# Five recurrent turns inside the last tile of the first projection, with the weights and buffers laid out for it

## The reference, cut to what matters

```python
def _layer_a(x, conv_buf, h0, norm_g, w_in, cw, cb, w_gx, b_gx, w_ga, b_ga, lam, w_out):
    u = _rmsnorm(x, norm_g) @ w_in               # first projection
    xb, gate = jnp.split(u, 2, axis=-1)
    xc, new_buf = _causal_conv(xb, conv_buf, cw, cb)
    h, h_last = _rglru(xc, h0, w_gx, b_gx, w_ga, b_ga, lam)      # recurrence
    y = (h * jax.nn.silu(gate.astype(jnp.float32))).astype(x.dtype) @ w_out
    return x + y, ...

def _rglru(u, h0, w_gx, b_gx, w_ga, b_ga, lam):
    uf = u.astype(jnp.float32)
    i_t = jax.nn.sigmoid(_block_diag(u, w_gx, b_gx).astype(jnp.float32))
    r_t = jax.nn.sigmoid(_block_diag(u, w_ga, b_ga).astype(jnp.float32))
    log_a = LRU_C * r_t * jax.nn.log_sigmoid(lam.astype(jnp.float32))
    a = jnp.exp(log_a)
    mult = jnp.sqrt(-jnp.expm1(2.0 * log_a))
    bx = mult * i_t * uf
    ...                                          # scan: h[t] = a[t] * h[t-1] + bx[t]
```

## Time and profile before

| | |
|---|---|
| median of 3 runs | 1619.05 us (1617.78 to 1621.24) |
| the profiled execution's own time | 1617.59 us |
| its span, first to last instruction | 1615.8 us |
| PE busy | 1513.2 us, 94% |
| DVE busy | 1159.9 us, 72% |
| ACT busy | 706.7 us, 44% |
| POOL busy | 336.3 us, 21% |
| mean granted TensorE clock | 0.978 of full speed |

### The profile page before, as it was taken

How to read it: one execution, slowest core, us unless ns; L and a number is a source line. 1 busy time by engine, 2 the same in 40 slices (tenths; PEclk the granted TensorE clock), 3 DMA queues, 4 the chain that set the end, 5 groups by cost and what they waited for, 6 DMA issues and landing times.

```text
span 1615.8 us, 31117 instructions
## 1 busy us (share of the span) xinstructions
PE 1513.2 (94%) x10752; PEld 1439.6 (89%) x10752; DVE 1159.9 (72%) x2212; ACT 706.7 (44%) x1576; POOL 336.3 (21%) x240
## 2 busy tenths in 40 slices
PE   7999999998499999998889999999996899999999
PEld 7999999998489999998879999999994688888888
DVE  7865565677499999998865846648457777777771
ACT  5322132134867667762334424334234444444440
POOL 0000000035565555554321000000122111111110
PEclk9999999999699999999899999999997999999999
DMA  6322122153223333334432212112523343333412
GB/s 239 116 81 68 64 85 67 58 174 112 86 85 106 105 97 103 109 92 158 147 104 72 76 51 81 54 62 76 164 85 104 94 116 92 108 88 102 117 47 79
DMA packets 161967, 158.45 MB, mean 98 GB/s; under 512 B 54832, under 2 KB 154928, under 8 KB 161840
## 3 DMA queue, kind: packets, MB, share of 16 engines
q1 hardware_dynamic: 149712, 147.44, 30.2%
q10 hardware_dynamic: 12128, 9.39, 1.8%
HBM read 102.68 MB, written 54.36 MB: 97 GB/s over the span
## 4 chain that ended last, share of the span: by engine, by line
PE 63%; DVE 18%; issue 7%; ACT 3%; DMA 3%; SPq 1%; POOL 1%; DVEq 0%; ACTq 0%; POOLq 0%
PE bank L651 19%; PE s_banks L651 19%; PE bank L1473 11%; DVE r_th L952 4%; PE s_banks L1410 3%; DVE r_x_hi L976 2%; PE bank L1425 2%; PE bank L1455 2%; PE bank L1213 2%; PE bank L1459 1%; PE bank L635 1%; DVE r_x L972 1%; PE s_banks L1182 1%; ACT m_p L1653 1%; DVE b_qstd L534 1%
## 5 line engine op out<-in xcount | busy, mean ns | idle before, releaser
L705 POOL TENSOR_TENSOR w_lo_a<-w_raw_a,w_hi_a 128x1024 fp32r<-128x1024 f32 x24 | 57.9, 2425 | 706.5 <-ACT w_hi_a L700 706.5
L1653 ACT ACTIVATE m_p<-s_banks,m_nm 128x192 f32<-128x192 f32 (+2 forms) x264 | 106.0, 414 | 182.9 <-DVE m_nm L1524 182.9
L1473 PE MATMUL bank<-m_y_hi,w_hi_a 128*128 128x256 f32 (+1 forms) x512 | 150.2, 293 | 0.6 <-DVE m_out L1584 0.6
L1473 PE MATMUL bank<-m_y_lo,w_hi_a 128*128 128x256 f32 (+1 forms) x512 | 145.5, 284 | 0.0
L1473 PE MATMUL bank<-m_y_hi,w_lo_a 128*128 128x256 f32 (+1 forms) x512 | 145.4, 284 | 0.0
L483 ACT ACTIVATE a_out<-a_out 128x352 f32<-128x352 f32 x48 | 24.0, 500 | 255.5 <-DVE a_out L573 255.5
L651 PE MATMUL bank<-a_hi,w_hi_a 128*128 128x352 f32 x384 | 126.1, 328 | 9.8 <-DVE w_lo_a L705 9.6
L651 PE MATMUL s_banks<-b_hi,w_hi_a 128*128 128x352 f32 x384 | 130.4, 340 | 0.0
L651 PE MATMUL bank<-a_hi,w_lo_a 128*128 128x352 f32 x384 | 124.7, 325 | 0.0
L651 PE MATMUL bank<-a_lo,w_hi_a 128*128 128x352 f32 x384 | 124.6, 324 | 0.0
L651 PE MATMUL s_banks<-b_lo,w_hi_a 128*128 128x352 f32 x384 | 124.1, 323 | 0.0
(11 more groups left out here) (204 smaller groups left out, 4909.5 us busy)
## 6 DMA issues: line engine op xcount, KB each, us to landing
w_raw_a<-weights_dram SPq DMA_DIRECT2D x32, 512.0 KB, 4.6
w_raw_b<-weights_dram SPq DMA_DIRECT2D x18, 512.0 KB, 4.2
sga_dram<-a_out SPq DMA_DIRECT2D x48, 176.0 KB, 1.9
r_xc<-xc_dram SPq DMA_DIRECT2D x32, 264.0 KB, 2.9
r_sg<-sga_dram SPq DMA_DIRECT2D x32, 264.0 KB, 2.8
r_x<-xT_dram SPq DMA_DIRECT2D x64, 132.0 KB, 2.2
x_dram<-r_x SPq DMA_DIRECT2D x64, 132.0 KB, 1.8
b_x<-x_dram SPq DMA_DIRECT2D x48, 176.0 KB, 2.3
```

The lines of the kernel that those rows point to most:

```text
L705: ops.tensor_tensor(low, raw, high.bitcast(F32), ALU.subtract)\
L1473: mm = nc.tensor.matmul(out_bank(ts, blk)[:, 0:width], w[pw][:, kt * P:(kt + 1) * P], (m.y_hi, m.y_lo)[px][tp][:, kt, 0:width], start=(n = ...
L1653: nc.scalar.activation(m.p[:, q, k, v0:192], s_banks[:, 2 * q + e, bp * 192 + v0:(bp + 1) * 192], ACT.Exp, bias=m.nm[:, q, k:k + 1], accum ...
```

## The change

`EARLY` now holds five turns: turn 0 behind step 2 of the last tile, 1 behind 6, 2 behind 8, 3 behind 11, 4 behind 13. DVE does each behind the step before (1, 5, 7, 10, 12), and turn 5 behind step 14. SP's loads for these turns are spread over the last tile (`second`, `third`, `fourth`). The low part of y of turn 5 on POOL waits until the projection's last matmul. There is one more weight place (`SLOTS_B` 7), so that unit `U_GATE` is loaded and split in the first tile; the recurrent buffers are ordered anew, with an 80-column gap. DVE splits 11 further units in the last tile, behind steps 5 to 15, and one more in the first tile; POOL keeps two, behind turns 6 and 7. The decay constants are made behind steps 10 to 15 of the first tile, in six parts. Of the second projection's 16 units, one goes into the new place early, and five instead of four are loaded at the end of the recurrent section.

```diff
-SLOTS_A, SLOTS_B, SLOTS_C = 8, 6, 2
+SLOTS_A, SLOTS_B, SLOTS_C = 8, 7, 2
...
-                if m.first_weights and isinstance(s, int) and s == 1 and j + 6 < VECTOR_UNITS:
+                if m.first_weights and isinstance(s, int) and s == 1 and j + 6 <= 2 * NB:
                     low_part(eng, nc.vector, m.unit + j + 6)
+                if m.first_weights and isinstance(s, int) and s == PN and j >= 5 and U_GATE + j - 4 < VECTOR_UNITS:
+                    low_part(eng, nc.vector, U_GATE + j - 4)
                 after(s, j)
...
-        VECTOR_UNITS = UNITS_IN_A
+        VECTOR_UNITS = U_GATE + 12
...
-        SLOTS_IN_B = (list(range(UNITS_GATE)) + list(range(UNITS_GATE + UNITS_KV, SLOTS_A + SLOTS_B))
-                      + list(range(UNITS_GATE, UNITS_GATE + UNITS_KV)) + [SLOTS_A + SLOTS_B, SLOTS_A + SLOTS_B + 1])
+        SLOTS_IN_A = [15, 16] + list(range(1, 15))
+        SLOTS_IN_B = [14, 0, 1, 2, 3] + list(range(6, 12)) + [4, 5, 12, 13, 15]
...
-        EARLY = {(PN, 9): 0, (PN, 13): 1}
+        EARLY = {(PN, 2): 0, (PN, 6): 1, (PN, 8): 2, (PN, 11): 3, (PN, 13): 4}
...
-            project_sync(eng, a1, {0: start})
-            start_gates()
+            def second():
+                load_branch(1, 0)
+
+            def third():
+                load_branch(1, 1)
+                load_gate(0, 2)
+
+            def fourth():
+                load_branch(1, 2)
+                load_gate(0, 3)
+
+            project_sync(eng, a1, {0: start, 1: start_gates, 7: second, 10: third, 12: fourth})
+            load_gate(1, 0)
             run_steps(eng, 2, RN - 2, RN + 2, body)
-            for u in range(U_B1 + UNITS_GATE + UNITS_OUT_A, U_OUT_B):
+            for u in range(U_B1 + UNITS_GATE + UNITS_OUT_A - 1, U_OUT_B):
                 load_unit(eng, u, r.kv_mm, NB * RN)
...
             def after_project(s, j):
-                if isinstance(s, int) and (s, j) == (PN, NB):
-                    decays(eng)
-                if isinstance(s, int) and (s, j) in ((PN, 7), (PN, 12)):
-                    turn(0, 0, 0 if j == 7 else 1)
+                if isinstance(s, int) and s == 1 and j >= 10:
+                    decays(eng, j - 10)
+                if isinstance(s, int) and (s, j + 1) in EARLY:
+                    early_turn(turn, EARLY[s, j + 1])
+                if isinstance(s, int) and (s, j) == (PN, 14):
+                    early_turn(turn, len(EARLY))
...
+                if isinstance(s, int) and (s, g) == (0, NG - 1):
+                    eng.wait_ge(a1.proj_done, 2 * NB * PN)
...
-            low_units(eng, U_GATE, U_GATE + 7)
-            turn(0, 0, 0)
-            low_units(eng, U_GATE + 7, U_GATE + 11)
-            turn(0, 0, 1)
+            for n in range(len(EARLY)):
+                early_turn(turn, n)
```

More of the change, by code:

```diff
@@ new lines, in decays @@
+            if part == 0:
+                eng.wait_ge(lw_act, 2)
+                step(1, nc.vector.tensor_scalar(tmp, e, 2.0, None, ALU.add))
+                step(2, nc.vector.reciprocal(tmp, tmp))
+                step(3, nc.vector.tensor_tensor(z, e, tmp, ALU.mult))
+                step(4, nc.vector.tensor_tensor(z2, z, z, ALU.mult))
+                step(5, nc.vector.memset(acc, 1.0 / (2 * LW_TERMS + 1)))
+            elif part <= LW_TERMS // 2:
+                for i in range(2):
+                    k = LW_TERMS - 1 - 2 * (part - 1) - i
+                    step(2 * i + 1, nc.vector.tensor_tensor(acc, acc, z2, ALU.mult))
+                    step(2 * i + 2, nc.vector.tensor_scalar(acc, acc, 1.0 / (2 * k + 1), None, ALU.add))
+            else:
+                step(1, nc.vector.tensor_tensor(acc, acc, z, ALU.mult))
+                step(2, nc.vector.tensor_scalar(tmp, vec[:, LAM, :], -1.0, 0.0, ALU.mult, ALU.max))
+                step(3, nc.vector.scalar_tensor_tensor(out=tmp, in0=acc, scalar=2.0, in1=tmp, op0=ALU.mult,
+                                                       op1=ALU.add))
+                nc.vector.tensor_scalar(neg_decay[:, :], tmp, -4.0, None, ALU.mult)
+                nc.vector.tensor_scalar(decay[:, :], tmp, 4.0, None, ALU.mult).then_inc(lw_step, 1)
@@ L782, in back_pair, with early_turn, run_recurrent @@
             return (t, 2 * pair) if known(s, lag, RN - 1 + lag) else None
-        EARLY = {(PN, 9): 0, (PN, 13): 1}
-        def run_recurrent(eng, turn, last, after=None):
+        EARLY = {(PN, 2): 0, (PN, 6): 1, (PN, 8): 2, (PN, 11): 3, (PN, 13): 4}
+        def early_turn(turn, n):
+            s, g = divmod(n, NG)
+            turn(s, s % 2, g)
+        def run_recurrent(eng, turn, done, last, after=None):
             def body(s, par):
                 for g in range(NG):
-                    if not (isinstance(s, int) and s == 0 and g < len(EARLY)):
+                    if not (isinstance(s, int) and NG * s + g < done):
                         turn(s, par, g)
@@ L853, in body @@
                         load_branch(s + 1, g - 2)
+                    if isinstance(s, int) and (s, g) == (RN - 1, 0):
+                        load_unit(eng, U_B1)
                     if isinstance(s, int) and (s, g) == (RN, 0):
-                        for k in range(UNITS_GATE):
+                        for k in range(1, 1 + UNITS_GATE):
                             load_unit(eng, U_B1 + k, r.gates_done, 4 * NG * RN)
@@ L859, in body @@
                         load_next(pair, 0)
-                    if known(s, 0, RN - 1) and not (isinstance(s, int) and s == 0 and g < 2):
+                    if known(s, 0, RN - 1):
                         load_gate(s, g)
@@ L887, in start @@
                 eng.wait_ge(a1.proj_done, 2 * NB * (PN - 1))
[L888 to L889 removed]
+                for j in range(4):
+                    eng.wait_ge(a1.stored[place(a1, j)], stored_before(a1, 2, j))
                 for g in range(NG):
```

70 lines of the change are left out of this document (28 added, 42 removed).

## The result

The changed kernel takes 1597.97 us in the median (1597.15 to 1599.24), against 1618.93 us for the kernel before (1617.78 to 1621.24) in runs on the same chip. The ratio is 0.9869 with a 95% interval of 0.9852 to 0.9887: 21 us faster, where the forecast was 12.

A forecast was written before the change was run, and what follows sets the result against it. The prediction took the stretch from 409 to 433 us as a chain of latencies, the gain being how much earlier DVE reaches turn 7. Terms -11.5 - 2.0 + 1.5 = -12.0 gave 1605.6, median 1607.0 us, range 1599 to 1614.

The forecast's parts named there:

- A: The forecast itself: DVE gets to turn 7 earlier, median 1607.0 us, 1603 to 1611 by its bounds; chance 0.62.
- the ring: Last tile, from turn 3 on: DVE and ACT each wait for the other in turn, 14.4 us a turn.
- everything moves as a block: Behind DVE's start of turn 7, all work shifts together up to the hand-over to the second projection; no further term.
- Reordered places elsewhere are free: Weight places reordered elsewhere cost nothing, each unit being loaded a turn or more ahead of its use; no term.
- POOL's remaining two splits stay in turns 6 and 7 as before: Turns 6 and 7: POOL's two remaining weight splits keep their turns; no term for them.
- First tile, +1.4: First tile: added split and decay operations on DVE make PE wait 1.4 us before step 15; bounds 0 to 2.1.
- The last tile, to turn 6, -11.5: Last tile of the first projection: DVE's `one_minus` of turn 6 begins 11.5 us earlier, the first tile's +1.4 included.
- the price of the lock on DVE: Last tile: POOL's instructions hold DVE through shared ports for about 2.3 us of the next steps per turn.
- Rival B: Last tile: PE sets the pace, as ring and lock cost less; in all -20.9, 1598 us; chance 0.12.
- Turn 6, -2.0: Turn 6: POOL's split of unit 11 moves to DVE in the tile and no longer slows the scans; -2.0 us.
- Hand-over, +1.5: Hand-over to the second projection: five weight loads instead of four before the small outputs; +1.5 us, bounds 0 to 4.6.
- rival D: Last tile: weights come late behind stores in SP's queue, margin 0.9 us; slower, 1627 us; chance 0.07.

The follow-up runs named there:

- first trace: The changed kernel's first profile, compared with the one trace of the kernel before: -20.5 us in sum; median 1597.97 us.
- the two traces: The changed kernel profiled, then the same program run again with no edit: -20.5 and -21.1 us against the kernel before; medians 1597.97 and 1597.28 us.

## Why the prediction was wrong

The mechanism of the forecast, A, holds: DVE gets to turn 7 earlier by the turns inside the tile, at the pace of the ring. The sum was wrong by 8.5 us between the traces (-12.0 against -20.5). The steps that failed stand behind turn 7: "everything moves as a block" and "Reordered places elsewhere are free", which put the end of the second projection at nothing where the traces have -4.1 and -2.3 us, and "POOL's remaining two splits stay in turns 6 and 7 as before", where turns 7 to 9 have -1.9 and -2.0. One by one:

- *First tile, +1.4.* PE waits 1.5 us before step 15, and the price is 1.4 at the third norm: right. By the last tile 0.7 of it are left, as each tile between is 0.25 us shorter. Why they are stays open; I had no term for it.
- *The last tile, to turn 6, -11.5.* Turn 6 started 12.6 us earlier in the first trace, 13.8 counted from the first norm. Of the 2.3 us that the forecast lacks, 0.7 are those of the first tile, 0.6 the wait for turn 0's low part (1.4 forecast, 0.81 at 339.57), and 0.9 lie between the ends of turns 2 and 3 on DVE (18.5 forecast, 17.6 measured).
- *The ring of DVE and ACT.* 14.4 us a round forecast, 14.3 measured. ACT's side sets it: DVE waits 1.8 us a round for the square, and its own work is 12.5, not 14.4, so the price of the lock on DVE was put too high. The forecast had both sides at 14.4; that one was wrong did not show in the time. The load of `r_xc`, to which I gave no term, keeps DVE waiting for 4.4 us before 425.71, but it then waits 2.3 more for the square, so the load does not set the time. Rival B, that PE sets the pace, gave nearly the right time for a wrong reason: turn 5 ends at 418.8, not at 411.0 (its 409.6 and the first tile's 1.4).
- *Turn 6, -2.0.* Turn 7 came a further 1.0 earlier, not 2.0. This miss and the one before it have opposite signs, and with the late start of the first trace they make the good match at turn 7. POOL's two remaining splits did not stay where they were on DVE's axis: before they stood in turns 7 and 8, as the starts at 453.67 and 466.28 show, and now in 6 and 7. Turn 6 keeps a split, turn 8 has none, and from turn 6 to 9 the gain is 2.9 us against the 2.0 forecast. That coming sooner saves nothing by itself is shown by the kernel with two turns and POOL's splits.
- *Hand-over, +1.5.* From the store of k to the landing of the last state store 16.1 us, before 15.2: +0.9, and 0.4 to 0.7 at the second norm. Right in place, and 0.8 to 1.1 too dear. I priced the fifth load and took the 7.2 us landing beside it for given; the run without that landing in the path is worth 10.9 us.
- *"Reordered places elsewhere are free"* and *"everything moves as a block"* failed at the end of the second projection: -4.1 and -2.3 us in the two traces, the largest miss in the first. I asked whether each unit is loaded in time, not what its load stands ahead of in SP's queue. The stores behind it gave DVE back 1.0 to 1.5 us. The rest goes with PE's clock, partly by chance; its cause is argued, not shown.
- *The median.* The difference between the profiled execution and the median (1.5) was carried over. It was 0.8 after, and the kernel before has single runs from 1611.92 to 1621.24, more than the 0.2% that I gave a measurement.

The rest, -1.5 in the last turns of the first trace, is within what traces of kernels that are the same there differ by, and no step of the forecast has to account for it. Three small slips of the working change nothing of this: the bounds given for A make 1604.1 to 1610.8, not 1603 to 1611; PE would be ready for turn 0 at 336.8, not 336.6; and in rival D the margin is used up by a landing of 5.5 us, not 6.

## What to carry to other kernels

When loads change places, read the queue for what stands behind each of them, not only for whether the load is in time: a store that an engine waits for took 4.0 to 4.3 us behind a 512 KB load here, and 1.8 with none ahead. A queue that waits for small stores to land before it goes on is worth a look ahead of any work on the engines; moving four of them gave 10.9 us, half of what the whole change gave. And a split on GpSimd has no fixed price: it cost 0.1 us where VectorE waited, and 2.1 where a scan or another operation with two inputs ran.

## What the runs showed of the hardware

A wait of PE can cost more than its length. After the wait of 7.3 us at the hand-over the first matmuls take 0.49 us in place of 0.32, with a granted clock of 0.58 from 810 to 815 us and 0.73 in the 5 us behind, and the whole hand-over shrank by 9.6 us when the wait of 7.3 went. At the start of the attention two executions of the same program differ by 1.8 us, and in the 20 us behind the first row maximum the granted clock is 0.83 in the one and 0.66 in the other. Before the first norm, 1.2 us of difference arise with a granted clock of 1.00 in every window: from 12 to 15 us PE starts 18 matmuls in the trace of before and 11 in that of after. What makes them was not found.
